# Attention outputs of the first half made transposed, two heads side by side, and softmax sums inverted by ScalarE after they are spread

## The reference, cut to what matters

```python
p = jnp.exp(s - m)
l = jnp.sum(p, axis=-1, keepdims=True)
if sink is not None:
    l = l + jnp.exp(sk - m)
o = jnp.einsum('bngrqk,bnkgd->bnqgrd', (p / l).astype(v.dtype), vv)
```

## Time and profile before

| | |
|---|---|
| median of 3 runs | 3646.11 us (3641.60 to 3654.21) |
| profiled execution | 3644.51 us, of which the span of the trace is 3642.6 us |
| granted TensorE clock, mean | 0.928 |
| TensorE busy | 3120.5 us (86%) |
| DVE busy | 1985.4 us (55%) |
| GpSimd busy | 1372.3 us (38%) |
| ACT busy | 716.2 us (20%) |

### The profile page before, as it was taken

The page is one execution under the profiler, slowest core; times in us unless marked ns, Lnnn a source line. Parts: engine busy times, 40 slices in busy tenths (PEclk is TensorE's granted clock), DMA queues, the critical chain, the costliest instruction groups (busy, mean ns, idle before and its releaser), DMA issues. The chain is left out here.

```text
span 3642.6 us, 45069 instructions
## 1 busy us (share of the span) xinstructions
PE 3120.5 (86%) x17368; PEld 2281.6 (63%) x17368; DVE 1985.4 (55%) x4127; ACT 716.2 (20%) x1760; POOL 1372.3 (38%) x1166
## 2 busy tenths in 40 slices
PE   8899988986768877567889968889998999998999
PEld 3566478852334444244678856678874788877887
DVE  2331345498898888776776688776643210132101
ACT  2221222222111111113320013220023210122100
POOL 0840032056777777653455765554600000000000
PEclk9898999998889989787799979899999999999999
DMA  7422100279999999977889999899930244422342
GB/s 218 130 76 67 52 3 3 61 272 361 362 370 365 387 370 393 361 288 245 281 322 403 404 358 360 289 346 403 402 98 26 79 151 154 146 82 82 117 152 102
DMA packets 379436, 832.18 MB, mean 228 GB/s; under 512 B 40467, under 2 KB 176590, under 8 KB 379214
## 3 DMA queue, kind: packets, MB, share of 16 engines
q0 software_dynamic: 147456, 536.94, 39.3%
q1 hardware_dynamic: 231766, 292.35, 23.9%
HBM read 827.02 MB, written 2.17 MB: 228 GB/s over the span
## 5 line engine op out<-in xcount | busy, mean ns | idle before, releaser
L2369 POOL DMA_INDIRECT arena<-in_peer_u,arena x512 | 587.0, 1147 | 430.7 <-DVE arena L2499 182.1
L2369 POOL DMA_INDIRECT arena<-in_peer_v,arena x512 | 596.7, 1165 | 356.2 <-DVE arena L2485 205.0
L2499 DVE CUSTOM_DVE_ANT_0 arena<-arena 128x1024 f32<-128x1024 f32 x512 | 628.2, 1227 | 175.4 <-DMA arena<-in_peer_u,arena 145.9
L2441 PE MATMUL banks<-arena 128*128 128x512 f32 x768 | 410.2, 674 | 197.4 <-ACT arena L2460 121.4
L3843 PE MATMUL banks<-arena 128*128 128x256 f32 x2560 | 557.5, 378 | 0.0
L3843 PEld LDWEIGHTS banks<-arena 128*128 128x128 f32 x2560 | 483.8, 189 | 70.4
L2822 PE MATMUL banks<-arena 128*128 128x256 f32 x2176 | 502.8, 389 | 22.8 <-DVE arena L2944 18.8
L2822 PEld LDWEIGHTS banks<-arena 128*128 128x128 f32 x2176 | 417.9, 194 | 99.4 <-issue 30.4
L2485 DVE SCALAR_TENSOR_TENSOR arena<-arena 128x1024 f32<-128x1024 f32 x316 | 406.3, 1286 | 85.9 <-DMA arena<-in_peer_v,arena 74.3
L2441 PEld LDWEIGHTS banks<-arena 128*128 128x128 f32 x768 | 155.0, 213 | 409.1 <-issue 247.4
L3878 PE MATMUL banks<-arena 128*128 128x256 f32 x1408 | 312.4, 382 | 22.3 <-DVE arena L3941 22.3
(11 more groups left out here) (320 smaller groups left out, 3561.5 us busy)
## 6 DMA issues: line engine op xcount, KB each, us to landing
arena<-in_l_w_gate SPq DMA_DIRECT2D x44, 1024.0 KB, 7.9
arena<-in_l_w_up SPq DMA_DIRECT2D x44, 1024.0 KB, 8.2
arena<-in_l_w_down SPq DMA_DIRECT2D x44, 1024.0 KB, 7.2
arena<-in_ada_w SPq DMA_DIRECT2D x24, 1024.0 KB, 7.7
arena<-in_l_w_qkv SPq DMA_DIRECT2D x24, 1024.0 KB, 8.6
arena<-in_w_in SPq DMA_DIRECT2D x33, 512.0 KB, 4.0
arena<-in_l_w_out SPq DMA_DIRECT2D x16, 1024.0 KB, 5.1
arena<-in_peer_q_w SPq DMA_DIRECT2D x10, 1024.0 KB, 12.2
```

What stands on the lines that cost most here:

```text
L2369: p.e.indirect_dma_start(e.ring[slot], None, tables[table], bass.IndirectOffsetOnAxis(ap=e.IDX[h][:, t, j:j + 1], axis=0)).then_inc(*p.up( ...
L2441: ins = p.e.matmul(k.bank[b], e.diag[x % 4], e.ring[slot][:, half * T:half * T + T], start=h == 0 and j == 0, stop=h == HEADS - 1 and j == ...
L2499: p.e.tensor_tensor_reduce(out=e.prod, in0=e.ring[slot], in1=e.H2[:, t, :], scale=1.0, scalar=0.0, op0=ALU.mult, op1=ALU.add, accum_out=e. ...
```

## The change

Both halves now follow the one order and the one way of half 1: no steps "output" and "store", and one step "outputs" per tile, issued at the next tile's first unit after its weights. The function that gave the early order is gone. In both halves no sum is inverted before it is spread: DVE adds the two parts of a sum where there are two (windowed units with their sink), and issues nothing for the others; TensorE spreads the sum itself; ACT takes the logarithm of the spread sums from bank 4 into `a.O` and then the exponential of minus that in place, and signals after the second. DVE's product now stores the tiles of half 0 too. ACT loads the logarithm's table after each gelu of the last two tiles of tokens.

```diff
--- before.py
+++ after.py
...
             h, t = dots
             p.wait_ge(S.dots_ready, (h, t, KN - 1))
             p.e.activation(e.AV[:, n % 2, :], e.AV[:, n % 2, :], ACT.Gelu_apprx_tanh).then_inc(*p.up(S.gelu_ready, (h, t)))
+            if t >= 2:
+                log_tables(p)
 
 
 def peer_dve(k, p):
...
         yield from self.take(10**6, 10**6)
 
 
-def late_order(units):
+def unit_order(units):
 
     n, former = len(units), None
     yield "scores", 0
...
     yield "outputs", former
 
 
+def two_sums(x):
+    return x.sink is not None or 0 < x.nb < x.m
+
+
 def group_of(units, u):
 
     return (u,) if units[u].w == P else (u - 1, u)
-
-
-def unit_order(units, late):
...
 def stores_of(k, a, name, units):
...
 
 
 def stored_by(k, a, tile):
-    return k.S.act_stored if a.h_id == 0 else k.S.dve_stored
+    return k.S.dve_stored
 
 
 def unit_cost(unit):
...
 
 def units_pe(k, p, a, name, units, fill, rate):
     S, filled, made = k.S, 0, set()
-    for step, u in unit_order(units, a.late):
+    for step, u in unit_order(units):
         x, key = units[u], (name, u)
         if step == "fill":
             filled = 0
...
             for j in range(x.m // P):
                 ins = p.e.transpose(k.bank[4][:, j * P:j * P + P], a.S[u % 2][:, j * P:j * P + P], k.ident)
             ins.then_inc(*p.up(S.weights_filled, key))
-        elif step == "output":
-            if filled < 4 * MM:
-                occupied(k, p, a, 1, 5)
-            p.wait_ge(weights_by(k, a, u), key)
-            p.wait_ge(*x.values_at)
-            p.claim(("bank", 5), S.act_scaled, key)
-            for j, values in enumerate(x.values):
-                ins = p.e.matmul(k.bank[5][:, 0:x.w], a.PT[u % 2][:, j * P:j * P + P], values, start=j == 0,
-                                 stop=j == len(x.values) - 1, skip_group_check=True)
-            ins.then_inc(*p.up(S.output_filled, key))
         elif step == "outputs":
             if filled < 4 * MM:
                 occupied(k, p, a, 1, 5)
...
                                      stop=j == len(x.values) - 1, skip_group_check=True)
                     if j == len(x.values) - 1:
                         ins.then_inc(*p.up(S.output_filled, (name, v)))
-            p.wait_ge(S.vector_step, ("inverted", *key))
+            if two_sums(x):
+                p.wait_ge(S.vector_step, ("summed", *key))
             p.claim(("bank", 4), S.act_scaled, key)
             for v in group:
                 y = units[v]
-                ins = p.e.matmul(k.bank[4][y.c0:y.c0 + y.w, 0:P], a.small[:, v % 4, 4:5].to_broadcast([P, y.w]), k.ident,
+                ins = p.e.matmul(k.bank[4][y.c0:y.c0 + y.w, 0:P], a.small[:, v % 4, 2:3].to_broadcast([P, y.w]), k.ident,
                                  start=True, stop=True, skip_group_check=True)
             ins.then_inc(*p.up(S.store_filled, key))
-        elif step == "store":
-            p.wait_ge(S.act_scaled, key)
-            p.claim(("bank", 4), stored_by(k, a, x.tile), key)
-            p.e.transpose(k.bank[4][:, 0:P], a.O[x.tile], k.ident).then_inc(*p.up(S.store_filled, key))
 
 
 def units_act(k, p, a, name, units, fill, rate):
     S, stored = k.S, {}
-    for step, u in unit_order(units, a.late):
+    for step, u in unit_order(units):
         x, key = units[u], (name, u)
         cols = a.small[:, u % 4, :]
         low = cols[:, 0:1]
...
                 p.wait_ge(S.output_filled, (name, u - 2))
             p.wait_ge(S.weights_filled, key)
             p.e.activation(a.PT[u % 2][:, 0:x.m], k.bank[4][:, 0:x.m], ACT.Copy).then_inc(*p.up(S.act_weights, key))
-        elif step == "output":
-            if x.c0 == 0 and x.tile in stored:
-                p.wait_ge(S.store_filled, stored[x.tile])
-            p.wait_ge(S.vector_step, ("inverted", *key))
-            p.wait_ge(S.output_filled, key)
-            p.e.activation(a.O[x.tile][:, x.c0:x.c0 + x.w], k.bank[5][:, 0:x.w], ACT.Copy, scale=cols[:, 4:5]).then_inc(
-                *p.up(S.act_scaled, key))
-            if x.ends:
-                stored[x.tile] = key
         elif step == "outputs":
             if x.tile in stored:
                 p.wait_ge(S.dve_stored, stored[x.tile])
             p.wait_ge(S.store_filled, key)
-            p.e.activation(a.O[x.tile], k.bank[4][:, 0:P], ACT.Copy).then_inc(*p.up(S.act_scaled, key))
+            p.e.activation(a.O[x.tile], k.bank[4][:, 0:P], ACT.Ln).then_inc(*p.up(S.scalar_step))
+            p.in_order()
+            p.e.activation(a.O[x.tile], a.O[x.tile], ACT.Exp, scale=-1.0).then_inc(*p.up(S.act_scaled, key))
             stored[x.tile] = key
-        elif step == "store":
-            p.wait_ge(S.store_filled, key)
-            p.e.activation(x.dst, k.bank[4][:, 0:P], ACT.Copy).then_inc(*p.up(S.act_stored, key))
 
 
 def units_dve(k, p, a, name, units, fill, rate):
     S = k.S
-    for step, u in unit_order(units, a.late):
+    for step, u in unit_order(units):
         x, key = units[u], (name, u)
         cols = a.small[:, u % 4, :]
         low = cols[:, 0:1]
...
             if x.sink is not None:
                 p.in_order()
                 p.e.tensor_tensor(low, low, x.sink, ALU.min).then_inc(*p.up(S.scores_low, key))
-        elif step == "weights" and a.late:
+        elif step == "weights":
             if weights_by(k, a, u) is S.dve_weights:
                 if u >= 2:
                     p.wait_ge(S.output_filled, (name, u - 2))
                 p.wait_ge(S.weights_filled, key)
                 p.e.tensor_copy(a.PT[1][:, 0:x.m], k.bank[4][:, 0:x.m]).then_inc(*p.up(S.dve_weights, key))
-            p.wait_ge(S.weights_exp, key)
-            if x.sink is not None or 0 < x.nb < x.m:
-                p.e.tensor_tensor(cols[:, 2:3], cols[:, 2:3], cols[:, 3:4], ALU.add).then_inc(*p.up(S.vector_step))
-                p.in_order()
-            p.e.reciprocal(cols[:, 4:5], cols[:, 2:3]).then_inc(*p.up(S.vector_step, ("inverted", *key)))
+            if two_sums(x):
+                p.wait_ge(S.weights_exp, key)
+                p.e.tensor_tensor(cols[:, 2:3], cols[:, 2:3], cols[:, 3:4], ALU.add).then_inc(*p.up(S.vector_step, ("summed", *key)))
         elif step == "outputs":
             p.wait_ge(S.output_filled, key)
             p.wait_ge(S.act_scaled, key)
             p.e.tensor_tensor(x.dst, k.bank[5][:, 0:P], a.O[x.tile], ALU.mult).then_inc(*p.up(S.dve_stored, key))
-        elif step == "output":
-            p.wait_ge(S.weights_exp, key)
-            if x.sink is not None or 0 < x.nb < x.m:
-                p.e.tensor_tensor(cols[:, 2:3], cols[:, 2:3], cols[:, 3:4], ALU.add).then_inc(*p.up(S.vector_step))
-            p.in_order()
-            p.e.reciprocal(cols[:, 4:5], cols[:, 2:3]).then_inc(*p.up(S.vector_step, ("inverted", *key)))
 
 
 def rotate_act(k, p, a, j, src, scale, key, rows=P, made=None):
```

More of the change, by code:

```diff
@@ L3095, in late_order @@
     yield "outputs", former
+def two_sums(x):
+    return x.sink is not None or 0 < x.nb < x.m
 def group_of(units, u):
     return (u,) if units[u].w == P else (u - 1, u)
-def unit_order(units, late):
-    if late:
-        yield from late_order(units)
-        return
-    n = len(units)
-    yield "scores", 0
-    ended = []
-    for u in range(n):
-        waiting, ended = ended, []
-        paired = both_halves(units, u + 1)
-        if u + 1 < n and not paired:
-            yield "scores", u + 1
-        for x in waiting:
-            yield "store", x
-        yield "fill", u
-        if paired:
-            yield "scores", u + 1
-        yield "weights", u
-        if u:
-            yield "output", u - 1
-            if units[u - 1].ends:
-                ended.append(u - 1)
-        yield "pause", u
-    yield "rest", 0
-    for x in ended:
-        yield "store", x
-    yield "output", n - 1
-    yield "store", n - 1
 def stores_of(k, a, name, units):
```

## The result

The changed kernel takes 3666.16 us (median of 9 runs, 3659.63 to 3678.11) against 3647.38 us of the kernel before (9 runs, 3631.82 to 3657.16): a ratio of 1.0054, with an interval of 1.0038 to 1.0070. It is slower by 19 us where 16 us less were forecast, and outside the range. The profiled execution has a span of 3664.4 us at a mean clock of 0.925.

What follows compares the result with a forecast made beforehand. It took half 0's attention to be bound by a loop through the queues, with no engine or transfer full. The terms -14 - 6 + 3 + 5 - 4 = -16 us gave a median of 3630 us, range 3605 to 3656.

Steps and rivals of the forecast that it cites:

- the one on DVE in half 0: DVE's queue in half 0: the product's wait for the exponential costs nothing in the first and dilated attention.
- Rival 3: DVE's queue in half 0: the waiting product blocks the peer's rows; +42 us, 3688, chance 0.14.
- TensorE in half 0: -14 and -6: Waits for scaling and store and 48 transposes go: -14 us in the first attention, -6 in the dilated one.
- +3 in cross attention: Half 0's cross attention, 16 tiles: DVE's product may stand behind a peer row; +3 us, between 0 and 10.
- the sign named for the spread product: If the forecast is right, the spread product has no wait over 1 us in half 0.
- The inverse on ACT: Both halves: logarithm equals the copy's 277 ns, exponential 311 ns; the way from spread to product grows by 0.34 us.
- Half 1: +5: Half 1: ACT's longer way, mostly in cross attention (+5.4), less missing inversions (-1.5), plus delayed copies (+1); between -2 and +12.
- Table loads: -4: Attention: seven table loads ahead of exponentials move to when ACT is mostly idle; -4 us, at most 9.
- rival 4: Loads behind the gelus delay ACT in the attention: 9 more, +11.5 us in place of -4; 3646, chance 0.05.
- rival 2: Half 0: DVE, not TensorE, sets the pace and the gain is swallowed; +1 us, 3647, chance 0.23.
- Rival 5: First attention of half 0: the clock rises from 0.68 to 0.9, up to 23 us less; 3607, chance 0.08.

## Why the prediction was wrong

**The step that failed** is the one on DVE in half 0: "In half 0 I cost it at nothing in the first and dilated attention, because DVE already waits 48.1 us for scores and 75.7 us for fetched rows there, and comes to the product later, past peer rows that half 1 does not have." The product waited 1.8 us a tile, and this wait cost 34 us (timed) to 39 us (profile), by the kernel without it. DVE's waits for scores were no cover: they vanished (60.7 to 3.4 us), but the waits of ACT for DVE's least grew by 41 us in their place. The reason is the order inside the queue: between the sum and the product DVE has no other work, and the peer row of the pause stands behind both (1697.11 to 1700.38 in the timeline). In the dilated attention a peer row let through by the filling can stand directly ahead, as the forecast had it, and the product still waits: 2.24 us at 2200.99, behind a row that ended at 2198.76. Free time summed over a stage says nothing about what stands at the place where the wait is put. The figure to read was the distance from DVE's last instruction ahead of the product to ACT's scaling, which is all on other engines.

**Rival 3** had the mechanism and the place, its sign (over 1.4 us a tile) came true with 1.8, and so did the lower DMA share. Its price of +42 was too high. It held 48.1 us for all that the new wait could replace, and overlooked the 12.6 us at the second line. The exchange was 86.1 us of new wait for 60.7 - 3.4 = 57.3 us of waits for scores, 29 us, in place of 96 for 48. I gave it 0.14 where the row from half 1, 2.84 us a tile, was the nearest row of the same instruction and spoke for it.

**TensorE in half 0: -14 and -6, +3 in cross attention.** The waits for scaling and store went as named, but the sign named for the spread product, no wait over 1 us, didn't come true: 32.4 us in 36 waits, the longest 4.5, where the terms took 22.3 us from half 1. The growth of the transposes' waits from 6.8 to 27.6 us (before at line 3206, now at 3182) had no term at all. With the product's wait away, half 0's attention is 21.4 us shorter than in the profile of before, beside the -14 - 6 + 3 - 4 = -21 that the terms give; with other profiles of the old half 0 as the measure it is 25. So the gain was there, and its sum well sized. That is partly luck, because its split was not: against the means of the old profiles it is -5 us in the first attention, -10 in the dilated one, and -4 and -6 in the cross attentions, for which I had put a loss. Nor was its content: I took the output products as unchanged, and their busy time in half 0 fell from 48.7 to 33.5 us (line 3215, now 3195), while the spread products cost 25.7 us where the transposes had cost 17.9, so 7.8 more and not 3.5. In the changed kernel itself the first cross attention lost 7 us and the second nothing that stands out (+1), for +3 in both: a mis-sized term, since they have the same wait at the product.

**The inverse on ACT.** Sized well: logarithm 278 ns (277 forecast), exponential 309 ns over the whole span (311). By the table of the Trainium skill (VectorE: DVE Perf Modes, "The TRN2 errata"), (224 + N) / 1.2 ns from SBUF, an estimate for 128 columns is 293 ns; the trace has 16 ns more. Both instructions, 1650 to 2440 us:

```profile
L3248 ACT ACTIVATE arena<-arena 128x128 f32<-128x128 f32 x48 | 14.9, 310 | 1.5
L3246 ACT ACTIVATE arena<-banks 128x128 f32<-128x128 f32 x48 | 13.3, 278 | 42.6 <-PE banks L3204 42.0 <-issue 0.6
```

**Half 1: +5.** Within its bounds, by the profiles +6 and by the timed kernel +10 (3 to 17). "Mostly in cross attention" was wrong: the two give 2.6 us, half of the 5.4 put there. A missing inversion on the way would explain that (8 x (0.34 - 0.157) = 1.5 us each, measured 1.3), but no run tests it. Most of the rest is in the first attention of half 1, 209 to 213 us in the five profiles with the new inverse against 203 to 210 in the five with the old. Part of that goes with the granted clock, which differs also between profiles with the same inverse. From 50 to 100 us into that stretch it was 0.97 in the two shortest (203 and 205 us, old inverse), 0.90 in the one with 209 us (new), 0.83 in two with 208 (old), and 0.80 in one with 210 (old) and in four with 212 to 213 (new). At 0.80 the two inverses are 3 us apart. Why the clock differed, the same code having 0.97 and 0.83, stays open.

**Table loads: -4, rival 4.** Not resolved by the runs (0.1% less, interval on both sides of zero); rival 4's +11.5 us for added loads lies outside what was measured (at most +0.1%, 3 us). The Trainium skill (ScalarE: Activation LUTs, "What ACT_TABLE_LOAD costs") puts a drain of about 1380 ns beside the load at every switch to a different set. By that the drains of nine more loads would be 12 us, an estimate; neither the time of this kernel (3 us at most) nor the row of a load shows such a cost.

**Rivals 2 and 5.** DVE's busy time didn't swallow the gain as rival 2 had it, since half 0 gets shorter as soon as the wait is away. Rival 5 did not occur: the clock of the first attention was 0.82 against 0.79, not 0.9.

## What to carry to other kernels

Before a waiting instruction is added to an in-order queue, look at the instruction just before it and ask how long the rest of the chain takes from there, not how much idle time the engine has in the stage: here 0.29 us of work held the queue for 1.8 us a tile and cost 34 us. Put it behind independent work that is anyway due (here the peer rows of one pause), and stop there: further back it delayed its own reader, by 10.9 us in the cross attentions. An order that fits a stage that runs alone (half 1) needs its waits looked at again before it is used beside other work.

## What I had not expected of the hardware

Two waits on different engines can be one. Taking a wait from DVE alone cut TensorE's waits for an unchanged ACT copy from 60.0 to 38.4 us. And the 192 output products of 64-wide heads in half 0 kept TensorE busy for 22.6 us when made transposed, the two heads of a tile one below the other, and for 38.9 us the old way, though a single one is no shorter (355 against 326 ns). Lastly, the same edit on ACT has a different worth by place: 0.62 us more on ACT's way per tile cost 0.67 us in cross attention and 0.26 us (4.2 over 16 tiles) in the dilated part of half 1.
